# All eight heads of the prompt's attention beside the recurrence's second tile, and the first expert pair's rows fetched from DRAM

## The reference, cut to what matters

```python
def wkv7(r, w, k, v, a, b, S0):            # layer 1, eight heads of 64
    def step(S, inp):
        r_t, w_t, k_t, v_t, a_t, b_t = inp
        sa = jnp.einsum('bhij,bhj->bhi', S, a_t)
        S = S * w_t[:, :, None, :] + sa[..., None] * b_t[:, :, None, :] + v_t[..., None] * k_t[:, :, None, :]
        return S, jnp.einsum('bhij,bhj->bhi', S, r_t)
...
def mla_block(q_lat, q_rope, q_pos, c, kr, k_pos):   # layer 1, eight heads, causal
    s = jnp.einsum('bqhc,bkc->bhqk', q_lat, c) + jnp.einsum('bqhr,bkr->bhqk', q_rope, kr)
    s = s.astype(jnp.float32) * MLA_SCALE
    s = jnp.where(k_pos[None, None, None, :] <= q_pos[None, None, :, None], s, -jnp.inf)
    pr = jax.nn.softmax(s, axis=-1).astype(c.dtype)
    return jnp.einsum('bhqk,bkc->bqhc', pr, c)
...
def hier_moe(x, P, l):                     # both layers
    lc = (xf @ P['moe_w_coarse'][l] + P['moe_b_coarse'][l]).astype(jnp.float32)
    pc = jax.nn.softmax(lc, -1)
    gsel = jnp.argmax(lc, -1)              # one of 4 groups
    lf = ...                               # 4 experts of that group
    tv, ti = lax.top_k(lf, FINE_TOPK)      # two of them
    ...
    h = jax.nn.silu(jnp.einsum('nd,edf->nef', xf, P['moe_w_gate'][l])) * jnp.einsum('nd,edf->nef', xf, P['moe_w_up'][l])
    y = jnp.einsum('nef,efd->nd', h * comb[..., None].astype(h.dtype), P['moe_w_down'][l])
```

## Time and profile before

| | us |
|---|---|
| median of three runs | 1005.51 |
| the three runs | 1005.51, 1009.14, 999.33 |
| the profiled execution's own time | 1004.75 |
| its span, first to last instruction | 1003.0 |
| mean granted clock of PE over the span | 0.891 of 2.4 GHz |

### The profile page before, as it was taken

The page is one execution under the profiler, slowest core; times in us unless marked ns, Lnnn a source line. Parts: engine busy times, 40 slices in busy tenths (PEclk is TensorE's granted clock), DMA queues, the critical chain, the costliest instruction groups (busy, mean ns, idle before and its releaser), DMA issues.

```text
span 1003.0 us, 20072 instructions
## 1 busy us (share of the span) xinstructions
PE 880.3 (88%) x8296; PEld 636.0 (63%) x8296; DVE 433.1 (43%) x975; ACT 237.3 (24%) x520; POOL 181.2 (18%) x216
## 2 busy tenths in 40 slices
PE   5894998796999999899969888889978969999994
PEld 3784776574756656687756666657755847466663
DVE  1697964615314333334942532433532154142434
ACT  0131222005011110435434221131650060101113
POOL 4104117000240001000018940000810002500000
PEclk9996998798899999899999876755889987899997
DMA  9652711153499998241000130000736444999901
GB/s 272 228 167 47 113 63 57 47 178 161 179 418 415 420 401 226 84 126 56 33 10 11 57 104 5 2 2 2 228 98 211 149 191 138 417 417 418 389 5 44
DMA packets 80249, 165.22 MB, mean 165 GB/s; under 512 B 20257, under 2 KB 58584, under 8 KB 71266
## 3 DMA queue, kind: packets, MB, share of 16 engines
q1 hardware_dynamic: 68348, 149.43, 41.6%
q0 software_dynamic: 6496, 13.93, 4.6%
q10 hardware_dynamic: 5312, 0.54, 0.5%
HBM read 155.70 MB, written 6.99 MB: 162 GB/s over the span
## 4 chain that ended last, share of the span: by engine, by line
PE 67%; DVE 16%; issue 5%; DMA 3%; POOL 3%; ACT 2%; ACTq 2%; SPq 1%; POOLq 0%; DVEq 0%
PE bank L2030 11%; PE bank L2074 6%; PE bank L2062 6%; PE bank L1648 6%; DVE scratch L2127 6%; PE bank L1918 6%; PE bank L809 3%; PE bank L666 2%; ACTq L2523 2%; PE bank L1867 2%; DMA scratch<-in_s_c_im 2%; PE bank L1862 2%; PE bank L2019 1%; SPq L2745 1%; PE bank L2009 1%
## 5 line engine op out<-in xcount | busy, mean ns | idle before, releaser
L1648 PE MATMUL bank<-x_fm,weight_slots 128*128 128x280 f32 x576 | 143.2, 410 | 4.2 <-ACT x_fm L2603 2.8
L2527 ACT ACTIVATE scratch<-bank 128x280 f32<-128x280 f32 (+5 forms) x118 | 55.8, 478 | 351.3 <-PE bank L2062 115.9
L1648 PEld LDWEIGHTS bank<-x_fm,weight_slots 128*128 128x128 f32 x576 | 112.1, 196 | 32.8 <-issue 4.6
L2030 PE MATMUL bank<-weight_slots,scratch 128*64 128x256 f32 x672 | 92.5, 379 | 0.0
L2030 PEld LDWEIGHTS bank<-weight_slots,scratch 128*64 128x64 f32 x672 | 58.6, 137 | 26.2 <-issue 4.6
L2127 DVE TENSOR_TENSOR scratch<-bank,scratch 128x256 f32<-128x256 f32 x16 | 6.8, 425 | 157.6 <-PE bank L2030 157.6
L2127 DVE TENSOR_TENSOR scratch<-scratch 128x64 f32<-128x64 f32 (+13 forms) x94 | 59.2, 649 | 31.6 <-ACT scratch L2527 29.2
L1918 PE MATMUL bank<-scratch,weight_slots 128*128 128x280 f32 x256 | 63.3, 410 | 4.9 <-DVE scratch L2127 4.9
L2074 PE MATMUL bank<-scratch 128*128 128x280 f32 x256 | 66.3, 406 | 1.4 <-ACT scratch L2527 1.4
L1918 PEld LDWEIGHTS bank<-scratch,weight_slots 128*128 128x128 f32 x256 | 50.0, 196 | 17.6 <-DVE scratch L2127 5.3
L2130 DVE TENSOR_TENSOR residual<-residual,bank 128x280 f32<-128x280 f32 x112 | 49.9, 445 | 23.9 <-PE bank L2074 19.2
(11 more groups left out here) (413 smaller groups left out, 1338.9 us busy)
## 6 DMA issues: line engine op xcount, KB each, us to landing
weight_slots<-in_moe_w_down SPq DMA_DIRECT2D x24, 1024.0 KB, 11.5
weight_slots<-in_moe_w_up SPq DMA_DIRECT2D x22, 1024.0 KB, 10.5
weight_slots<-in_moe_w_gate SPq DMA_DIRECT2D x20, 1024.0 KB, 10.4
scratch<-in_moe_w_gate SPq DMA_DIRECT2D x12, 1024.0 KB, 9.1
scratch<-in_moe_w_up SPq DMA_DIRECT2D x10, 1024.0 KB, 10.6
weight_slots<-in_od_w_in SPq DMA_DIRECT2D x9, 1024.0 KB, 5.6
weight_slots<-in_ev_w_in SPq DMA_DIRECT2D x8, 1024.0 KB, 14.8
scratch<-in_moe_w_down SPq DMA_DIRECT2D x8, 1024.0 KB, 12.2
```

The lines of the kernel that those rows point to most:

```text
L1648: ins = pe.matmul(b[:, 0:NT], w[:, k, P * m2:P * m2 + P], src[:, k, :], start=(k == 0), stop=(k == kt - 1))
L2030: ins = pe.matmul(b[CAP * j:CAP * j + CAP, 0:DE], XG[:, q % 2, k, CAP * j:CAP * j + CAP], w[j][:, k, :], start=(k == 0), stop=(k == KD - 1))
L2527: return act.activation(dst, b[:rows, 0:width], f, **kw).then_inc(ring.free, 1)
```

## The change

**In the recurrence.** A running counter takes the place of `j`. All calls of `beside` in tile 1 count, and nine new ones are put in: one behind the products `akt`, one between `t` and `t_last` in levels 0 to 2, one between `ta` and `tv`, and one in each of the four chunks behind `state`. Tile 1 then has 26. Tile 2 no longer carries parts of heads; `latent_queries` stays at k = 11 and `new_scores` at k = 12. ACT's copy of `AK` moves ahead of the attention's part at k = 2. PE, DVE and ACT change alike.

**In the experts.** `pack`, `XTM3`, the copies of `PICK` to four partition groups (with DVE's wait for them) and the table `before32` are gone. Pair 0 goes the way of the others: `rows_of_slots(0, 1)`, a cast, an indirect DMA, `turn(0)`. On DVE `row_numbers(0, 1)` stands between dispatch(0) and dispatch(1), `row_numbers(1, 4)` behind dispatch(1), and the capacity test and the weights' arithmetic behind dispatch(3). `x_rows` has three transfers instead of six.

```diff
+            points = itertools.count()
+
+            def beside(tt, k=None):
+
+                if tt == 1:
+                    h, part_ = divmod(next(points), HEAD_POINTS)
                     if part_ == 0 and 0 < h <= MH:
                         probs_turned(h - 1)
                     if part_ == 0 and h < MH:
                         scores(h)
                     if part_ == 1 and 0 < h <= MH:
                         attend(h - 1)
-                    if j == 29:
+                elif tt == 2:
+                    if k == 12:
                         new_scores()
...
+                beside(tt)
                 for lt, rt in ((BTF, RTF), (KTF, RTF)):
...
                     if lev < 3:
                         in_chunks(V.claim(), TTM, own(XX), WC, "t")
+                        beside(tt)
                     in_chunks(V.claim(), XX, own(TTM), WC, "t_last")
...
-                for rt, name in ((ATK, "ta"), (AK, "tv")):
-                    in_chunks(V.claim(), TTM, per_head(rt), WD, name)
+                in_chunks(V.claim(), TTM, per_head(ATK), WD, "ta")
+                beside(tt)
+                in_chunks(V.claim(), TTM, per_head(AK), WD, "tv")
                 beside(tt, 10)
...
                     close(V, ins, "state")
+                    beside(tt)
...
             def beside(tt, k=None):
 
                 r = PT[tt][1]
+                if tt > 0 and k == 2:
+                    plain(AK[:r, :], 512, r)
+                if tt == 1:
+                    h, part_ = divmod(next(points), HEAD_POINTS)
...
-                pool.wait_ge(ev("rows_out"), 48 + 96 * (l + 1))
-                for q in range(1, NQ):
-                    if q in (1, 4):
+                pool.wait_ge(ev("rows_out"), 48 + 48 * (l + 1))
+                for q in range(NQ):
+                    if q in (0, 1, 4):
                         pool.wait_ge(*mark[f"rows{l}_{q}"])
                     if q == 4:
                         weights_of(l, 0)
-                    if q >= 5:
+                    if q >= 4:
                         pool.wait_ge(ev(f"rows_in{q % 4}"), rows_landed(l, q - 4))
...
                 def rows_of_slots(q0, q1):
 
-                    pe.wait_ge(ev("dispatch_ready"), NG * l + (q1 - 1) // 2 + 1)
                     b = V.claim()
                     for q in range(q0, q1):
+                        pe.wait_ge(ev("dispatch_ready"), NG * l + q // 2 + 1)
...
-                pack(0, 0)
-                pack(0, 1)
+                rows_of_slots(0, 1)
                 rows_of_slots(1, 4)
+                turn(0)
...
-                dve.wait_ge(ev("pick_spread"), 3 * l + 3)
...
                 dispatch(0)
+                row_numbers(0, 1)
+                dispatch(1)
+                row_numbers(1, 4)
+                dispatch(2)
+                dispatch(3)
                 s.do(dve.tensor_reduce(CNT[:, 0:1], CNT, AX.X, ALU.max))
...
-                dispatch(2)
-                dispatch(3)
                 packed(0)
-                row_numbers(1, 4)
...
-                act.wait_ge(ev("pick_ready"), l + 1)
-                for c in range(1, 4):
-                    act.activation(PICK[32 * c:32 * c + TT[2][1], 2, :], PICK[0:TT[2][1], 2, :], ACT.Copy).then_inc(ev("pick_spread"), 1)
...
-                for t in range(2):
-                    sp.dma_start(x_dram[P * t:P * t + P, :], XTM[:, t].rearrange("p k f -> p (k f)")).then_inc(ev("rows_out"), 16)
-                for c in range(4):
-                    sp.dma_start(x_dram[2 * P:NT, :].rearrange("r (half c f) -> c r half f", half=2, c=4)[c], XTM3[32 * c:32 * c + TT[2][1]]).then_inc(ev("rows_out"), 16)
+                for t, (c0, r) in enumerate(TT):
+                    sp.dma_start(x_dram[c0:c0 + r, :], XTM[:r, t].rearrange("p k f -> p (k f)")).then_inc(ev("rows_out"), 16)
```

More of the change, by code:

```diff
@@ L14 @@
+import itertools
 import math
@@ L430, in rows_landed @@
         def rows_landed(l, q):
-            return 16 * sum((m, k) <= (l, q) for m in range(2) for k in range(1, NQ) if k % 4 == q % 4)
+            return 16 * sum((m, k) <= (l, q) for m in range(2) for k in range(NQ) if k % 4 == q % 4)
         kt_read, score_banks = {}, {}
```

78 lines of the change are left out of this document (25 added, 53 removed).

## The result

| | median of the changed kernel | median of before, run beside it | ratio |
|---|---|---|---|
| 12 executions each | 1012.27 us (1005.88 to 1019.40) | 1004.24 us (999.33 to 1013.64) | 1.0085 (95%: 1.0056 to 1.0114) |

The account below looks back on a forecast made before the run. The prediction took the matmul engine, busy for 88% of the span, as the bound. Points -4.9 and experts +6.0 gave +1.1 on the profiled execution's 1004.75: 1005.9, stated as 1006.0 us, range 995 to 1014.

Parts of the forecast that it names:

- Tile 2 loses 19.0 us: Recurrence, third token tile: without the parts of three heads it falls from 46.8 to 27.8 us.
- Tile 1 gains 15.7 - 1.6 = 14.1 us: Recurrence, second token tile: two scores, three turns and three attends add 15.7 us, filled idle time takes off 1.6.
- Idle time that the denser points can fill, -1.6: Tile 1: half of PE's 3.1 us of waits behind L809 and before L680 gets filled, new waits a few tenths.
- part 1: Attention points moved from tile 2 into tile 1 of the recurrence: -4.9 us, bounds -10 to +1.
- rival C: Tile 1's clock stays low throughout, slowing the 44% of the tile at the high clock: whole +12, 1017 us; chance 0.09.
- The base: Starting point: one profiled execution of 1004.75 us, with tile 1 at 78.4 us and a granted clock of 0.72.
- Part 2's chain: Experts' start, dispatch through row numbers, cast, gather and turn to the gate: 10.95 us; +0.7 layer 0, -0.3 layer 1.
- Rival B: Experts: the first gather lands at today's median of 8.8 us, making the whole +8.9, 1013.6 us; chance 0.14.
- Part 2's clock price of 2.8 each: Each layer's gate restarts at the low clock after PE idles: 2.8 us added per gate, bounds 0 to 3.5.
- Rival D: Only the points in the recurrence work as summed and the gate's clock price is absent: 1000 us; chance 0.17.
- Part 2 as a whole: Experts, first pair's rows gathered instead of packed, both layers with the clock price: +6.0 us, bounds -1.0 to +15.
- Rival A: PE's clock rises in tile 1 and the gates start warm: 996 us; chance 0.15.

Follow-up runs that it names:

- e7: Kernel before, with the attention of all eight heads in one block in front of tile 2's first point, tiles 1 and 2 otherwise bare: 1037.6 ± 3.0 us.
- e8: e1 plus one dense matmul in front of each group of chunk products in tile 2: 1016.4 ± 3.4 us.
- e5: Kernel before with only the experts' change, and DVE's cast of row numbers for pairs 1 to 3 moved behind dispatch(3): 998.6 ± 1.3 us.
- e3: e1 plus one more attention point in tile 1, between the re and gc products (27 points): 1003.2 ± 1.5 us.
- e1: Kernel before with only the change of the recurrence and its attention points, experts as before: 1009.7 ± 1.1 us.
- e12: e9 plus one more attention point in tile 1, behind the re products (27 points): 1002.6 ± 1.2 us.
- e9: The whole changed kernel, with DVE's cast of row numbers for pairs 1 to 3 moved behind dispatch(3): 1006.5 ± 1.1 us.
- e4: e3 with a head's pieces reordered to attend, scores, then the turn of the probabilities: 1008.7 ± 2.5 us.
- e10: e5 with three more points in tile 1, so six heads there and two left to tile 2: 1007.7 ± 1.9 us.
- e11: e5 with the first three points of tile 1 empty, so four heads there and four left to tile 2: 1008.0 ± 1.0 us.

## Why the prediction was right and wrong

- **Tile 2 loses 19.0 us: right.** 46.0 to 27.3 on the means of the profiles, 18.7; bare 27.8 in e7 to the tenth.
- **Tile 1 gains 15.7 - 1.6 = 14.1 us: the step that failed.** Measured 24.1 (72.0 to 96.1), 10.0 more. By the forecast's own prices the part in front of the first state product was to grow by 1.25 + 3.5 + 2 x 1.65 - 1.6 = 6.4 us; it grew by 9.5, with the new wait of 3.2 (1.3 in e8) in it. Behind it, two turns, a set of scores and an attend were to cost 2 x 1.25 + 3.5 + 1.65 = 7.7; it grew by 14.6. There PE is busy 25.8 us against 9.7 in e5, and the pieces that came are 2 x 1.05 + 2.2 + 1.13 = 5.4 us at e5's full-clock durations, so 10.7 us are the price of 0.50 in place of 1.00 on everything in that stretch, of which the forecast's mixed prices held 2.3. Filling the empty gap (e3 against e1, e12 against e9) takes 6 of the 10 us away again; the clock is then 0.66 in the stretch, and falls after the wait of 2.0 us for probabilities. (e4 has the gap filled too, but its waits for ACT bring tile 1 back to 97.0.) The other 4 are not assigned; they are within what four profiles of one code differ by.
- **"Idle time that the denser points can fill, -1.6": wrong in sign.** PE's idle time in tile 1 went from 9.5 to 15.2 us. The wait behind the chunk products did go, as said, but the softmax chain got too little time (L680 1.3 to 6.3 us; "a few tenths" was said), and one point fell empty where scores had stood. The prediction counted 26 points and never asked which part of a head lands on each: 17 points (0 to 16) stand before the one at k = 12, so it is point 17 = 5 x 3 + 2, the part that has nothing on PE. Before it was point 12, in e3 and e12 it is 18, in e10 15, in e11 9: all multiples of three, with a turn and scores, and none of them has the wait.
- **The sizes of the pieces, and the clock.** The bounds of part 1 took the moved pieces at either clock, 11 to 18.2 us, but not the work that was already there. That was rival C alone, at 0.09; its mechanism (the part of the tile at the high clock slows) is what happened, in the last 27 us and not throughout. Its sum, part 1 at +6, is close to the +5.6 to +9.4 measured.
- **The base.** The forecast took 78.4 us for tile 1 from one execution; three others with the same code gave 67.5, 69.9 and 72.3. That execution had also begun faster (router copy of layer 0 at 238.3 us; 239.3 to 244.3 in the other thirteen), so its total looked typical. Its window at 0.72 could not show that the tile had a high clock to lose.
- **Part 2's chain.** Gate 11.97 us behind dispatch where 10.95 was summed. In layer 0 the gather was issued 3.8 us behind dispatch (3.25 said), the landing took 4.4 us (4.9 said; 5.0 in layer 1), and the turn with its copies 3.7 (2.8 said): the last is DVE. The prediction had the numbers of pairs 1 to 3 "at about 255.3", 5.5 us behind dispatch, and they came 7.1 us behind it, because one-column matmuls were costed at their full-clock duration; it did not follow what is queued on DVE behind that cast. Rival B (landing at 8.8) is out: 4.4 and 5.0.
- **Part 2's clock price of 2.8 each: 2.8 measured in layer 1, 1.5 in layer 0.** The agreement in layer 1 is in part luck: before's own profile has 14.1 us there, and e1 with the same experts 13.1, against which the price is 3.9. Rival D (no price) is out for this stretch. The rule that the prediction weighed, from the Trainium skill's page "TensorE: Matmul & The Clock Gate", section "HAM oscillation — how this bites in real kernels", is that PE pays for a wait with the low clock on its next burst. The gates behind the gather agree with it (8.58 and 9.53 us against 7.13), and so does the wait of 3.2 us in tile 1, though on DVE and not on a DMA, where what paid was the remaining 27 us.
- **Part 2 as a whole.** Dispatch to first down is 6.7 us longer in the two layers together, against 6.0 forecast. But the whole kernel shows only -1.2 ± 2.3 (on before) and +2.5 ± 1.6 (on the points). Some 4 to 8 us of what the gates lose is missing in the end. It is not in a stretch that follows them directly (first to last down 115.8 and 115.6 us, 115.9 and 116.1 before). With the experts of before, only one profile has five heads in tile 1, so whether tile 1 itself is shorter behind the new experts, or that profile was an odd one, stays open.
- **The total** came inside the range by luck, because two misses met: part 1 at some +7.6 (the mean of 5.6, 7.9 and 9.4) is 12 over its forecast, part 2 at some +1 (between -1.2 and 2.5) is 5 under it. Rival A, by which the clock rises in tile 1, is out: its mean clock fell from 0.81 in the four profiles with five heads to 0.73 in the four with 26 points. That was not foreseen, and the range was wide enough only because of the rivals.

## What to carry to other kernels

When work is threaded between the steps of a chain, write down which piece lands at each step before and after, and look for the step that is left with nothing on the engine that sets the pace: here filling one empty point in 26 gave back 6 us of the tile, a quarter to a third of it idle time and the rest the clock of the same matmuls. Bound a clock effect over the whole stretch that it can reach, not over the pieces that move, and look at more than one execution of that stretch. And when an engine has to wait for a slow producer, put what does not depend on it ahead of that wait: one moved line gave 4 to 6 us, while neither part of the change gained anything clear of noise.

## What the runs showed of the hardware

- The same matmuls of tile 1 (some 1637 records) took 67.5, 69.9, 72.3 and 78.4 us in one profile each of four kernels that share this code, with the granted clock at 0.88, 0.85, 0.78 and 0.72.
- After one wait of 3.2 us the clock stood at 0.50 for 27 us though PE was busy 25.8 of them. With the place of the wait filled it came back to 1.00 there (after 6.8 us at 0.50 without a pause), and fell again after the next wait of 2.0 us. In e8 a wait of 1.8 us, 8 us before the stretch, had the same 27 us at 0.50 behind it.
- Dense matmuls of the whole array did not raise it: 14 spread over 38.6 us (0.54), or two in 3.8 us with a third of 1.2 us some 4 us later (0.50).
- Matmuls of one column took 0.24 us a record at the low clock (24 in 5.85 us) and 0.14 us at the high one (24 in 3.44 us); a wait for them is longer than their work suggests.
